# Mean square of the convolution mixer: squares added by GpSimd, one matmul, placed one weight unit later

## What is computed

```python
h = rmsnorm(x, mix_norm)
z = h @ w_in                       # 2048 -> 3584
y = concat([fourier_mixer(z[..., :512]), spatial_gating_mixer(z[..., 512:1536]),
            short_conv_mixer(z[..., 1536:3072]), multiscale_pool_mixer(z[..., 3072:])])
y = rmsnorm(y.reshape(b, s, 4, 512), out_norm)      # each mixer's 512 channels by themselves
x = x + y.reshape(b, s, 2048) @ w_out
h = rmsnorm(x, ffn_norm)
x = x + hierarchical_moe(h, ...)   # 32 experts, top 2, gated MLP of width 768
out = rmsnorm(x, final_norm)
```

## Time and profile before

| | |
|---|---|
| median of three runs | 2032.17 us |
| the profiled execution | 2030.56 us |
| its span in the trace | 2029.0 us |
| TensorE matmul busy | 1868.2 us, 92% of the span |
| VectorE busy | 590.4 us, 29% |
| GpSimd busy | 248.4 us, 12% |
| ScalarE busy | 178.4 us, 9% |
| mean granted TensorE clock | 0.962 of full speed |

### The profile page before, as it was taken

How to read it: one execution, slowest core, us unless ns; L and a number is a source line. 1 busy time by engine, 2 the same in 40 slices (tenths; PEclk the granted TensorE clock), 3 DMA queues, 4 the chain that set the end, 5 groups by cost and what they waited for, 6 DMA issues and landing times.

```text
span 2029.0 us, 21000 instructions
## 1 busy us (share of the span) xinstructions
PE 1868.2 (92%) x9478; PEld 1067.6 (53%) x9478; DVE 590.4 (29%) x834; ACT 178.4 (9%) x258; POOL 248.4 (12%) x100
## 2 busy tenths in 40 slices
PE   8999999999969999899988999988899989999895
PEld 7887878788844444444344444434444444434342
DVE  3221656611142222222222223222222312222224
ACT  4000110100110000000000010000001000000003
POOL 4333535433300000000000000000000000000001
PEclk9999999999979999999999999999999998899998
DMA  7222233443289999999999999999999999999994
GB/s 274 83 78 83 64 103 89 180 173 104 108 318 424 429 430 429 429 429 430 431 428 430 429 430 430 429 430 430 429 430 429 429 429 429 428 431 429 430 428 182
DMA packets 67419, 681.13 MB, mean 336 GB/s; under 512 B 10304, under 2 KB 13568, under 8 KB 40320
## 3 DMA queue, kind: packets, MB, share of 16 engines
q1 hardware_dynamic: 64464, 671.16, 79.3%
q0 software_dynamic: 2304, 8.39, 1.0%
q10 hardware_dynamic: 560, 0.21, 0.0%
HBM read 679.73 MB, written 8.39 MB: 339 GB/s over the span
## 4 chain that ended last, share of the span: by engine, by line
PE 55%; DMA 42%; DVE 1%; issue 0%; ACT 0%; DVEq 0%
DMA region_rest<-in_w_gate 23%; PE banks L1055 20%; PE banks L735 15%; DMA region_w<-in_w_gate 9%; PE banks L929 9%; DMA region_h<-in_w_gate 6%; PE banks L1046 4%; PE banks L1076 3%; DMA region_w<-in_w_up 3%; PE banks L966 1%; PE banks L813 1%; PE banks L825 1%; PE banks L762 1%; PE banks L1031 1%; DMA region_h<-x_rows,region_rest 1%; PE banks L728 0%
## 5 line engine op out<-in xcount | busy, mean ns | idle before, releaser
L1055 PE MATMUL banks<-region_rest,region_w 128*64 128x384 f32 x2432 | 416.1, 496 | 54.3 <-DMA region_rest<-in_w_gate 43.3
L1055 PEld LDWEIGHTS banks<-region_rest,region_w 128*64 128x64 f32 x2432 | 181.9, 139 | 280.2 <-issue 214.0
L1503 DVE TENSOR_TENSOR region_x<-banks,region_x 128x1024 f32<-128x1024 f32 x128 | 151.1, 1220 | 601.3 <-PE banks L1046 600.9
L735 PE MATMUL banks<-split_h,split_w 128*128 128x512 f32 x864 | 273.7, 394 | 0.5 <-DVE split_w L1159 0.5
L1076 PE MATMUL banks<-region_rest,region_w 128*64 128x512 f32 x936 | 232.9, 655 | 15.4 <-DVE region_w L1529 13.0
L458 POOL TENSOR_TENSOR split_w<-region_rest,split_w 128x2048 fp32r<-128x2048 f32 x42 | 196.8, 4685 | 307.4 <-DVE split_w L1166 307.4
L735 PEld LDWEIGHTS banks<-split_h,split_w 128*128 128x128 f32 x864 | 162.2, 188 | 35.2 <-issue 0.7
L513 POOL DMA_INDIRECT region_h<-x_rows,region_rest x16 | 16.0, 1001 | 1271.2 <-PE banks L1031 1260.1
L735 PE MATMUL banks<-split_w 128*128 128x512 f32 x432 | 168.2, 389 | 0.0
L929 PE MATMUL banks<-split_w,split_h 128*128 128x512 f32 x512 | 160.0, 394 | 0.0
L1055 PE MATMUL banks<-region_h,region_w 128*64 128x384 f32 x832 | 143.1, 498 | 18.2 <-DMA region_h<-in_w_gate 12.4
(11 more groups left out here) (209 smaller groups left out, 1169.9 us busy)
## 6 DMA issues: line engine op xcount, KB each, us to landing
region_rest<-in_w_gate SPq DMA_DIRECT2D x40, 3072.0 KB, 31.1
region_rest<-in_w_down SPq DMA_DIRECT2D x38, 3072.0 KB, 31.0
region_rest<-in_w_up SPq DMA_DIRECT2D x36, 3072.0 KB, 30.6
region_h<-in_w_up SPq DMA_DIRECT2D x14, 3072.0 KB, 30.0
region_w<-in_w_up SPq DMA_DIRECT2D x14, 3072.0 KB, 29.7
region_w<-in_w_down SPq DMA_DIRECT2D x13, 3072.0 KB, 31.0
region_h<-in_w_gate SPq DMA_DIRECT2D x12, 3072.0 KB, 31.0
region_w<-in_w_gate SPq DMA_DIRECT2D x12, 3072.0 KB, 31.0
```

The source lines that it names most:

```text
L735: mm = t_.matmul(ps[:, 4 * (c % 2) + m, :], w[s][:, kk, cols_m], h[:, k, :], start=(k == 0 and w is w_hi and h is h_hi), stop=(k == KT - 1 ...
L1055: mm = t_.matmul(ps[h * SLOTS:(h + 1) * SLOTS, u, 0:HF], hTe[:, k, :], ring_gu[slot][:, kk, h * HF:(h + 1) * HF], start=(k == 0), stop=(k ...
L1503: v.tensor_tensor(tile, ps[:, 2 + 2 * c:4 + 2 * c, :], tile, ALU.add).then_inc(comb_added, 1)
```

## The change

In GpSimd's list, three additions of squared tiles are put behind the subtraction for unit 30. In TensorE's list, the mean square of the convolution mixer becomes one matmul of the sum, as for the other mixers, and it moves from between units 28 and 29 to between units 29 and 30. The lists of VectorE, ScalarE and SyncE stay as they are.

```diff
@@ gpsimd
-                if u in (16, 17, 24):
+                if u in (16, 17, 24, 30):
                     for m in (1, 2, 3):
-                        sum_squares((16, 17, 24).index(u), m)
+                        sum_squares((16, 17, 24, 30).index(u), m)
@@ tensor
             def mean_square(nth, bank):
-                if nth < CONV:
-                    pe.wait_ge(sq_summed, 3 * nth + 3)
-                    t_.matmul(ps[:, bank, :], mean_w, sq[nth][:, 0, :], start=True, stop=True).then_inc(ms_ps, 1)
-                    return
-                for m in range(NH):
-                    pe.wait_ge(sq_ready, NH * nth + m + 1)
-                    mm = t_.matmul(ps[:, bank, :], mean_w, sq[nth][:, m, :], start=(m == 0), stop=(m == NH - 1))
-                mm.then_inc(ms_ps, 1)
+                pe.wait_ge(sq_summed, 3 * nth + 3)
+                t_.matmul(ps[:, bank, :], mean_w, sq[nth][:, 0, :], start=True, stop=True).then_inc(ms_ps, 1)
@@ tensor
             pe.wait_ge(rms_ready, 3)
             out_unit(28)
+            out_unit(29)
             mean_square(CONV, 0)
-            for u in (29, 30, 31):
+            for u in (30, 31):
                 out_unit(u)
```

## The result

The changed kernel takes 2035.2 us, the median of 22 runs (2033.14 to 2036.79), against 2031.96 us for the kernel before (22 runs, 2030.38 to 2035.02). The ratio is 1.0015 with a 95% interval of 1.0009 to 1.0021: +3.24 us, slower by 0.15%. No change (1.0000) lies outside the interval; the 0.2% that the prediction took as its bound for a change lies above the measured value and just inside the interval. The forecast was +3.67 us and 2035.8.

A forecast was written before the change was run, and what follows sets the result against it. TensorE was taken to bound the edited stage, followed by the experts' weight stream. Terms -2.57 (matmuls), +4.55 (wait and restart) and +1.69 (clock) gave +3.67 us, 2035.8 against the median; range 2032.8 to 2038.2.

The forecast's parts named there:

- What bounds: Output projection: TensorE works without a gap; the experts' weight stream begins after its last unit, so shifts reach the end whole.
- Removed: Convolution mean square on TensorE: 3.43 us becomes 0.86 with one matmul, giving TensorE 2.57 us.
- Added: GpSimd's three additions behind unit 30's subtraction: 4.02 us, hidden by 0.9 us behind TensorE's unit 29.
- The other end: Upper case for GpSimd's additions: 5.13 us, as beside a working VectorE, holding TensorE up by 0.2 us.
- Moved: Mean square ends 8.31 us later, delaying root, normalization, unit 31's cast and subtraction; TensorE stalls some 4.2 us before unit 31.
- The restart: Unit 31's first matmul after the wait ends 0.50 us after its start instead of adding 0.23: 0.27 us.
- The clock: First part of unit 31 after the stall: TensorE at the lower clock costs 1.69 us, from 0 to 3.4.
- The sum: Whole kernel: -2.57 for matmuls, +4.55 for wait and restart, +1.69 for clock, giving +3.67 us.
- rival 1: Stall before unit 31, but the clock stays up or is soon back: +1.98 us, 2034.2; chance 0.13.
- (2): Restart of unit 31: clock needs twice the ordinary time, price 3.4 us, total +5.4, 2037.5; chance 0.13.
- (3): Before unit 31: no stall comes and the 2.57 us are kept, 2029.6 us; chance 0.04.
- (4): Expert stage: TensorE's slack there takes the shift up, near 2032.2 to 2033 us; chance 0.08.

The follow-up runs named there:

- e6: Kernel before with 18 useless matmuls (4.1 us at full clock) ahead of the output projection's last weight unit, 43: 2036.59 us, ratio 1.0021.
- e5: Kernel before with squares added behind GpSimd's subtraction for unit 29 and the one-matmul mean square inside unit 29, after 12 matmuls: 2029.6 us, ratio 0.9986.
- e3: Changed kernel with VectorE's cast for unit 31 put ahead of the convolution mixer's normalization: 2029.77 us, ratio 0.9983 against the kernel before.
- e7: Changed kernel with GpSimd's additions behind the subtraction for unit 29 instead of unit 30: 2035.47 us, ratio 1.0016 against the kernel before.
- e2: Kernel before with GpSimd's additions behind the subtraction for unit 29 and a one-matmul mean square left between units 28 and 29: 2029.89 us, ratio 0.9988.
- e4: Changed kernel with 18 useless matmuls between units 30 and 31, in place of the stall: 2032.92 us, ratio 1.0005 against the kernel before.
- e8: The changed kernel run once more, unaltered, against the kernel before: 2035.21 us, ratio 1.0015.
- e1: Kernel before with the mean square, still four matmuls and without GpSimd's additions, moved behind unit 29: 2037.96 us, ratio 1.0027.

## Why the prediction was right, step by step

- **What bounds.** TensorE without a gap, then a stream that TensorE's last unit holds back. Held: e6 passed a shift of 4.1 us through to the end, and between unit 31 and unit 43 TensorE has no wait, before or after. The stream does not begin as a whole behind the last unit, as the prediction put it: two transfers are issued before, and the third is the one that waits for that unit.
- **Removed, -2.57 us.** The mean square took 0.87 us, and e5 and e3, in which nothing else is late, stand at -2.55 and -2.50 by the yardstick.
- **Added.** 4.02 us forecast for the additions, 4.03 measured, nobody waiting (e7). The other end, 5.13 beside a working VectorE, came true in e2 with 5.09.
- **Moved.** Root at 391.33 forecast and 391.45 measured, where the whole trace lies 0.15 later than the one before; reciprocal, multiplications and low parts back to back as in the earlier trace rows; the cast at 400.55 and 400.63; the subtraction's end at 406.42 and 406.49. The stall was forecast at 4.2 us and measured at 4.20. That one cast's place decides it is shown by e3. The last rows of x, which the prediction had landing shortly before their reader, held nobody up: the third addition of x began at 416.71, behind TensorE as before.
- **The restart.** 0.27 us forecast. In e4, where the clock stays up, units 31 and 32 take 22.05 us, where two units take 21.77: 0.28.
- **The clock, 1.69 us.** 1.62 by e4 against the changed kernel, 1.55 by e8. That the price of a pair of rows in the experts' stage holds here too was assumed; it came out to 0.1. The Trainium skill's TensorE: Matmul & The Clock Gate (Why this matters for your kernels) advises against idle gaps between bursts; the traces of the change, of e1, e7 and e8 agree, with four stalls of 4.1 to 4.2 us and a granted clock below 1.00 behind each.
- **The sum.** +3.67 forecast. In the trace unit 31 counts from 406.54 - 0.15 + 0.27 = 406.66 against 404.75, so +1.91 for the order; with 1.62 for the clock that is +3.53, and the yardstick says +3.54. Two small terms make the difference: the subtraction took 4.50 us instead of 4.59, and the clock 1.62 instead of 1.69.
- **The time.** +3.24, with an interval of +1.8 to +4.3; the forecast lies inside, and the yardstick too. So does rival 1's +1.98: the time alone doesn't tell the two apart, the windows and e4 do. The chance of a third that it would come out above 0.2% allowed for 0.8 us of spread in the clock's price and the runs; the clock's price came out within 0.1 to 0.2 us.
- **The rivals.** The clock did not stay up (1) and did not need twice the time here (2), though a fall at twice the price does occur (e4, last section); the stall came (3); the experts' stage took nothing up (4).

**What the prediction read wrongly.** It says that three of its four rows of waits in the experts' stage agree with the advice against idle gaps. In those rows the clock was lost behind waits of 2.69 and 3.20 us and kept behind waits of 1.93 and 3.04. More rows of the same trace of before show that the length of the wait alone does not decide it there:

```profile
839.18 7.08 PE L1055 MATMUL banks<-region_rest,region_w 128*64 128x384 f32 x32 [2.03 <-DMA region_rest<-in_w_gate]
...
1377.34 5.38 PE L1055 MATMUL banks<-region_h,region_w 128*64 128x384 f32 x32 [2.03 <-DMA region_h<-in_w_gate]
```

For a wait of 4.2 us the prediction had no row. That the clock would fall was its likelier case, and it fell in four traces of four.

## What to carry to other kernels

A step that another engine's hand-written list stands behind is priced by what is queued behind it, not by its own length: here 2.6 us of matmuls were saved and 6.1 us lost, because one cast of 1.2 us stood behind the normalization in VectorE's list. Before moving a step later, write down for each engine what its list holds behind that step and when the receiver needs it; if a gap results, move the innocent instruction ahead (here into a gap in which VectorE waited anyway). And allow for the lower clock behind a stall of TensorE: here it came behind each stall of 4.1 to 4.2 us and cost 1.6 us more, while waits of 2 to 3 us in the experts' stage were followed by it only in part.

## What the runs showed that was not expected

**The clock also falls in or right behind the router's matmuls.** In the output projection, TensorE multiplies by the router's weights for 3.49 us at a time, 32 records of 36 columns (L966), without a gap. Within or right behind some of these stretches the granted clock falls below 1.00, although TensorE did not wait. In the kernel before, the chain of waits shows the third column block at 34.35 us for 144 matmuls where the second takes 32.77, and the windows show the clock:

```profile
442.66 32.77 PE banks L929 x144
...
488.10 3.49 PE banks L966 x32
491.60 34.35 PE banks L929 x144
```

```profile
490.00:495.00 5.00, 5.00 (x25) 4.24 (x25) 0.31 (x1) 0.00 (x0) 4.05 (x1) 0.70 0.00 0
```

This costs 1.58 us. It happened once in the traces of before, of the change, of e1, e2, e4, e7 and e8, and twice in e3, e5 and e6, at different ones of the three router stretches. Each time it cost about 1.6 us, only in e4 3.2, with the granted clock at 0.50 from 445 to 451 us. A term of about 1.6 us that comes once or twice is as large as the differences studied here, and it is why e3 stands at -2.50 behind unit 32 but its weight stream starts only 0.9 us earlier than before. What decides how often it comes was not tried, nor whether the narrow matmuls bring it or something that stands around them.

**A cast waits for GpSimd whole.** The cast for unit 32 began 0.46 us into GpSimd's subtraction and took 5.12 us instead of 1.23 (5.06 to 5.23 in e1, e4, e7 and e8): it ended 1.1 us after the subtraction did, in all five traces. The same shows behind another GpSimd instruction: in e2 and e7 the cast for unit 30 begins during the last of the three additions, takes 2.04 us and ends 1.1 us after it. In e7 that addition ends at 380.62:

```profile
379.67 2.04 DVE L1161 CAST split_w<-region_rest 128x2048 fp32r<-128x2048 f32 x1 [0.18 <-PE banks L923]
```

The 1.1 us are nearly the cast's whole length of 1.23. The late cast for unit 32 was off the path here: GpSimd had unit 32 ready at 407.65 + 4.59 = 412.24, and TensorE ended unit 31 near 430.21 - 10.885 = 419.3.
